# A fused decoder trunk on one core: VectorE's order in the differential heads, and what TensorE runs in the last two

## The chip, the cores and the metric

The kernel runs on one core of a Trainium2 chip. The metric is the device time of one execution in microseconds (us). Of the kernel before, three timed runs are shown: 712.58, 714.68 and 714.70, median 714.68 us.

## The reference

`x` is (1, 512, 1024) in float32, and the trunk has two layers.

```python
# layer 0: stick-breaking attention, 16 heads of 64
q, k, v, gate = split(rms_norm(x, g) @ w_in, 4)
x = x + (silu(gate) * stick_breaking_attention(q, k, v)) @ w_out
# shared keys and values of layer 1
k, v = split(rms_norm(x, kv_norm_g) @ w_kv, 2)       # 8 heads, keys 2 x 64, values 128
k = rope(rms_norm(k, k_norm_g))
# layer 1: differential attention
q, gate = split(rms_norm(x, g) @ w_in, 2)
q = rope(rms_norm(q, q_norm_g))
p = softmax(causal(q @ k.T / 8))                     # two maps (c = 0, 1) for each head
o = (p[0] - lam * p[1]) @ v
o = rms_norm(o, subln_g) * (1 - lam_init)
x = x + (silu(gate) * o) @ w_out
```

## The kernel before, in words

**Numbers.** Every matmul operand is kept as a rounded part (`_hi`) and the rest (`_lo`), and each product is three matmuls: hi x hi, hi x lo, lo x hi (`three`, L568 to L572). Weights come from HBM in slabs of 128x512. SyncE issues the loads (`slab`, L345), and each slab is split into hi and lo: GpSimd does both parts, or, for the slabs in `ACT_HI`, ScalarE the hi part (`slab_hi`, L935) and GpSimd the lo part (`split`, L464). In the differential stage the slabs stand in a ring of four slots (`RING_B`), so a slab can be split only when TensorE has used the slab four before it (semaphore `s_wu`), and loaded only when the slab four before it has been split (`s_w`).

**Stages.** First the stick-breaking layer, then the shared keys and values, then the differential stage (from L790 on TensorE), which is where the change lies. It has eight heads h = 0 to 7, each a pass over one 128-column block. Heads 0 and 1 stand apart, heads 2 to 5 are a loop (L896), heads 6 and 7 stand apart again (`late_head`, L879), and then comes the output projection (`project_out`, L730): 16 slabs `H_OUT` to `H_OUT + 15`, for each slab four tiles of 128 rows, eight output tiles in all.

**TensorE in head h of the loop** (`head`, L853): the scores of both maps into banks 0 to 5 (`scores_b`, L790); the q projection of head h + 2 into bank 6, and between its two slabs the spread of the output norms' roots of head h - 2 into bank 7 (`o_roots`, L812); the probabilities times values of head h - 1 into bank 7 (`attend_before`, L844, which waits for `s_og`, that is for VectorE's `o_scale(h - 2)`); the gate projection of head h into bank 6, and between its two slabs the sums of squares (`sums`, L756, which wait in `s_ot` for `o_times_gate(h - 1)`) and the transposes of the combined probabilities of head h (`turn_probs`, L820, which wait in `s_cm`). In heads 6 and 7 no q projection is left (`late_head`): scores, roots, attend, gate projection, sums, transposes.

**VectorE in head h** (`head`, L1544), in this order:

```python
for b in range(3): # maxima of a bank's scores from PSUM, then the bias of the exponentials (L1554, L1559)
q_add(h + 2)            # L1511, needs the swap of halves by four small DMAs (swap_halves, L400)
gate_log(h + KT)        # L1310
o_scale(h - 2)          # L1535, needs o_roots
combine((3, 2), 2, 4)   # L1572 to L1577: reciprocal, ratio, two strips of 512 and 384 columns
gate_silu(h + KT)       # L1316, then a wait for its own end (st.link)
q_low(h + 2)            # L1516
o_times_gate(h - 1)     # L1541, needs silu and ScalarE's output_square
combine((0, 1), 0, 8)   # strips of 128 and 256 columns, releases turn_probs
keep_hi(h - 2, ...); keep_lo(h - 2, ...)   # L1326, L1332: the gated output, split, for the projection
# mean squares, a root with ScalarE, Newton steps, then at_lo x3 (L1600), q_rotate(h + 3) (L1504, L1505)
```

`at_lo` of head h releases the scores of head h + 1 (`s_al`, L796).

**ScalarE in head h** (`head`, L1196): copy and absolute value of the gate from bank 6, exp and log of it (`gate_parts`, L1189, which waits for `s_ot`); the exponentials of bank 0; `q_square`; those of banks 2 and 3; `q_round`, which waits for `q_add`; `gate_exp`, which waits for `gate_log`; those of the last banks; `q_copy`; `output_square` (waits for attend, `s_pv`); the root; three copies of the transposed probabilities (L1223).

**GpSimd in head h**: the split of k for the next head (`key`, L521), two slab splits, the split of v (`value`, L526), two slab splits. A split is a cast (L479 or L493) and a subtraction (L481 or L495). At the end its order is H_OUT, H_OUT + 1, `value(7)`, H_OUT + 2 and the rest (L559 to L563).

Where the text gives a time as T6 + 5, T6 is the start of the scores of head 6. The functions that the diff touches, with the line numbers of the profile:

## Time and profile before

| | us |
|---|---|
| median of three runs | 714.68 |
| the profiled execution | 713.42 |
| its span in the trace | 712.0 |
| TensorE busy | 653.8 (92% of the span) |
| VectorE busy | 430.1 (60%) |
| ScalarE busy | 329.4 (46%) |
| GpSimd busy | 340.4 (48%) |
| mean granted clock of TensorE | 0.966 of full |
| chain that ended last: TensorE / VectorE / issue / ScalarE | 62% / 23% / 7% / 5% |

The span is what lies between the first and the last instruction; the execution's own time has 1.4 us more. A share of busy time is a mean over stages with different limits, so the argument goes stage by stage. A matmul's row shows its start and an overlapping duration; the distance from one start to the next is what it costs.

### The profile page before, as it was taken

What the parts mean: (1) busy time and instruction counts of PE and PEld (TensorE: products, weight loads), DVE (VectorE), ACT (ScalarE), POOL (GpSimd) and SP (SyncE); (2) the same over time, 40 slices, a digit from 0 to 9 for tenths busy, and PEclk for the clock granted to TensorE, in tenths of its full rate; (3) what the DMA queues carried; (4) which work ended last, traced back from release to release, by engine and by line L of the source; (5) the groups of instructions that cost most, each with busy time, mean ns of one, the idle gap of its engine ahead of it and who ended that gap; (6) DMA issues with size and microseconds to landing.
All of it is one profiled execution on the core that took longest, in us unless ns stands there. A gap on an engine that the chain in (4) does not pass through costs nothing.

```text
span 712.0 us, 10029 instructions
## 1 busy us (share of the span) xinstructions
PE 653.8 (92%) x3388; PEld 548.7 (77%) x3388; DVE 430.1 (60%) x683; ACT 329.4 (46%) x714; POOL 340.4 (48%) x325
## 2 busy tenths in 40 slices
PE   5999989999999999859798999998999889778898
PEld 4788778888888888758687888886877778667786
DVE  3400274775957758474937398237888998775421
ACT  4330555474754756632416544333654556443420
POOL 5554665544554442442551454558654574252241
PEclk9999999999999999989999999999999999876999
DMA  6222221212112110004121222233221111220241
GB/s 236 89 90 73 75 83 38 73 44 59 53 42 66 44 59 29 0 1 129 55 94 40 98 100 90 89 89 104 62 58 51 52 44 45 71 64 2 58 142 65
DMA packets 61773, 49.08 MB, mean 69 GB/s; under 512 B 7728, under 2 KB 48816, under 8 KB 61744
## 3 DMA queue, kind: packets, MB, share of 16 engines
q1 hardware_dynamic: 61744, 48.71, 22.5%
q8 instruction: 17, 0.28, 0.2%
q14 instruction: 12, 0.10, 0.0%
HBM read 44.50 MB, written 2.10 MB: 65 GB/s over the span
## 4 chain that ended last, share of the span: by engine, by line
PE 62%; DVE 23%; issue 7%; ACT 5%; DMA 2%; SPq 1%; DVEq 0%; ACTq 0%
PE bank L570 16%; PE bank L571 16%; PE bank L572 16%; PE bank L683 6%; DVE small L1554 3%; DVE hi L1354 3%; DVE lo L1359 2%; DVE sp L1348 2%; PE bank L668 2%; DVE ge L1310 1%; ACT ex L1027 1%; PE bank L807 1%; DVE ex L1435 1%; DMA xs<-in_x 1%; DVE v L1278 1%
## 5 line engine op out<-in xcount | busy, mean ns | idle before, releaser
L469 POOL TENSOR_TENSOR w_lo<-w_raw,w_hi 128x512 fp32r<-128x512 f32 x60 | 81.6, 1366 | 135.0 <-ACT w_hi L940 135.0
L481 POOL TENSOR_TENSOR w_lo<-w_raw,w_hi 128x512 fp32r<-128x512 f32 x100 | 139.0, 1390 | 8.0
L570 PE MATMUL bank<-w_hi,h_hi 128*128 128x512 f32 x320 | 128.6, 402 | 6.9 <-DVE xs L1416 4.1
L570 PE MATMUL bank<-h_hi,w_hi 128*128 128x512 f32 x320 | 131.4, 411 | 3.3 <-ACT q L1122 3.3
L479 POOL CAST w_hi<-w_raw 128x512 fp32r<-128x512 f32 x100 | 68.4, 684 | 131.9 <-PE bank L572 84.7
L571 PE MATMUL bank<-h_lo,w_hi 128*128 128x512 f32 x320 | 128.1, 400 | 0.0
L572 PE MATMUL bank<-h_hi,w_lo 128*128 128x512 f32 x320 | 127.7, 399 | 0.0
L572 PE MATMUL bank<-w_hi,h_lo 128*128 128x512 f32 x320 | 126.5, 395 | 0.0
L571 PE MATMUL bank<-w_lo,h_hi 128*128 128x512 f32 x320 | 126.1, 394 | 0.0
L940 ACT ACTIVATE w_hi<-w_raw 128x512 fp32r<-128x512 f32 x60 | 37.2, 627 | 90.0 <-PE bank L572 74.0
L570 PEld LDWEIGHTS bank<-w_hi,h_hi 128*128 128x128 f32 x320 | 61.1, 191 | 20.2 <-DVE xs L1416 4.5
L570 PEld LDWEIGHTS bank<-h_hi,w_hi 128*128 128x128 f32 x320 | 62.1, 194 | 16.9 <-ACT q L1122 3.9
L572 PEld LDWEIGHTS bank<-h_hi,w_lo 128*128 128x128 f32 x320 | 61.7, 193 | 14.0
L572 PEld LDWEIGHTS bank<-w_hi,h_lo 128*128 128x128 f32 x320 | 60.8, 190 | 13.4
L571 PEld LDWEIGHTS bank<-h_lo,w_hi 128*128 128x128 f32 x320 | 61.8, 193 | 11.9
L571 PEld LDWEIGHTS bank<-w_lo,h_hi 128*128 128x128 f32 x320 | 61.1, 191 | 12.4
L1348 DVE SCALAR_TENSOR_TENSOR sp<-bank,ex 128x512 f32<-128x512 f32 (+1 forms) x48 | 28.4, 591 | 47.5 <-ACT ex L1032 47.5
L1204 ACT ACTIVATE pr<-bank,small 128x512 f32<-128x512 f32 (+3 forms) x64 | 38.8, 614 | 11.8 <-DVE small L1559 11.8
L1365 DVE TENSOR_TENSOR lo<-ex,hi 128x512 fp32r<-128x512 f32 (+1 forms) x48 | 39.0, 866 | 7.4 <-ACT hi L1040 7.4
L683 PE MATMUL bank<-hi,neg_tri 128*128 128x512 f32 (+1 forms) x64 | 23.6, 380 | 14.5 <-DVE lo L1359 14.5
L1022 ACT ACTIVATE ex<-bank 128x512 f32<-128x512 f32 (+1 forms) x48 | 25.3, 528 | 23.3 <-PE bank L668 22.6
L1359 DVE TENSOR_TENSOR lo<-sp,hi 128x512 fp32r<-128x512 f32 (+1 forms) x48 | 35.4, 738 | 0.6
(175 smaller groups left out, 1220.7 us busy)
## 6 DMA issues: line engine op xcount, KB each, us to landing
w_raw<-in_a_w_in SPq DMA_DIRECT2D x64, 256.0 KB, 2.7
w_raw<-in_w_kv SPq DMA_DIRECT2D x32, 256.0 KB, 3.0
w_raw<-in_b_w_in SPq DMA_DIRECT2D x32, 256.0 KB, 2.8
w_raw<-in_a_w_out SPq DMA_DIRECT2D x16, 256.0 KB, 3.0
w_raw<-in_b_w_out SPq DMA_DIRECT2D x16, 256.0 KB, 2.9
xs<-in_x SPq DMA_DIRECT2D x4, 512.0 KB, 5.3
qrot<-qs SPq DMA_DIRECT2D x32, 64.0 KB, 2.0
out_x<-xs SPq DMA_DIRECT2D x8, 256.0 KB, 2.7
```

What stands on the lines that cost most here:

```text
L469: nc.gpsimd.tensor_tensor(w_lo[s][:, :], w_raw[s][:, :], w_hi[s][:, :].bitcast(F32), ALU.subtract).then_inc(s_w, 1)
L479: nc.gpsimd.tensor_copy(w_hi[s][:, :], w_raw[s][:, :]).then_inc(s_whi, 1)
L481: nc.gpsimd.tensor_tensor(w_lo[s][:, :], w_raw[s][:, :], w_hi[s][:, :].bitcast(F32), ALU.subtract).then_inc(s_w, 1)
L570: pe.matmul(o, ahi, bhi, start=start, stop=False, skip_group_check=True)
L571: pe.matmul(o, ahi, blo, start=False, stop=False, skip_group_check=True)
L572: return pe.matmul(o, alo, bhi, start=False, stop=stop, skip_group_check=True)
L683: mm = pe.matmul(bank[3 * h + b][:, cols(c, n)], (neg_tri if i == j else neg_one)[:, :], part[h][:, cols(STRIP[i][0], n)], start=False, st ...
L940: A(w_hi[s][:, :], w_raw[s][:, :], ACT.Copy).then_inc(s_whia, 1)
L1204: A(pr[c][:, cols(at, w)], bank[BANK_B[c, b]][:, cols(at - BANKS[b][0], w)], ACT.Exp, bias=tiny[:, 8 + 2 * i + c:9 + 2 * i + c], scale=mea ...
L1348: STT(out=sp[m // 3][:, seg], in0=bank[m][:, 0:BANKS[m % 3][1]], scalar=0.0, op0=ALU.max, in1=ex[m // 3][:, seg], op1=ALU.add).then_inc(s_ ...
L1359: TTN(lo[h][:, seg], sp[h][:, seg], hi[h][:, seg].bitcast(F32), ALU.subtract).then_inc(s_sl, 1)
L1365: TTN(lo[h][:, seg], ex[h][:, seg], hi[h][:, seg].bitcast(F32), ALU.subtract).then_inc(s_al, 1)
```

## The change

- VectorE's order in a head is now: maxima and biases, `o_scale`, `gate_log`, `combine((3, 2))`, `q_add`, `gate_silu`, `combine((0, 1))`, `o_times_gate`, `q_low`, `keep_hi`, `keep_lo`, and the rest as before. `gate_silu` no longer waits for its own end; it counts in a new semaphore `s_si`, for which `o_times_gate`, the stick-breaking layer's `gated_a` and ScalarE's `gate_parts` wait.
- ScalarE does `q_round` after the last exponentials and `q_copy`, and `gate_exp` earlier by that.
- In head 6 TensorE runs gate projection 6 before attend, and gate projection 7 behind the sums, with the transposes of head 6 between its slabs. In head 7 it runs no projection of a gate; in its place the first four slabs of the output projection are run tile by tile (`early_tile(0)` to `(3)`), each over k = 0 to 3, between the other steps. The output tiles have banks of their own (`OUT_BANK_B`), so no output tile waits for VectorE's addition.
- GpSimd splits the slabs H_OUT to H_OUT + 3 before `value(7)`.
- ScalarE and VectorE take their steps for gates 6 and 7 at the new places (`later`, `gate=False`). In head 6 ScalarE's `gate_parts(6)` stands ahead of `q_round` and `output_square`, and waits for `gate_silu(14)`.

The diff, cut to its core:

```diff
@@ -556,10 +560,10 @@
         value(KT - 2)
-        split(H_OUT)
-        split(H_OUT + 1)
+        for g in range(H_OUT, H_OUT + RING_B):
+            split(g)
         value(KT - 1)
-        for g in range(H_OUT + 2, N_ALL):
+        for g in range(H_OUT + RING_B, N_ALL):
             split(g)
@@ -587,15 +591,15 @@
-        def bulk_step(g, n0, k, src_hi, src_lo, freed, first):
+        def bulk_step(g, n0, k, src_hi, src_lo, freed=None, first=0, banks_of=range(8), tiles=range(TT)):
...
             whi, wlo = w_hi[slot_of(g)][:, :], w_lo[slot_of(g)][:, :]
-            for t in range(TT):
-                if k == 0 and n0 + t >= 6:
+            for t in tiles:
+                if freed and k == 0 and n0 + t >= 6:
                     pe.wait_ge(freed, first + n0 + t - 5)
-                mm = three(bank[(n0 + t) % 6][:, :], src_hi[:, k, cols(t * P, P)], src_lo[:, k, cols(t * P, P)],
+                mm = three(bank[(n0 + t) % 6 if freed else banks_of[n0 + t]][:, :], src_hi[:, k, cols(t * P, P)], src_lo[:, k, cols(t * P, P)],
                            whi, wlo, start=(k == 0), stop=(k == KT - 1))
...
@@ -876,17 +880,12 @@
-        def late_head(h, g, q=None):
-            scores_b(h, False)
-            o_roots(h - 2)
-            attend_before(h, 2)
-            pe.wait_ge(s_gc, h + KT)
-            pe.wait_ge(s_ga, h + KT)
-            project(g, h1_hi, h1_lo, bank[6][:, :])
-            sums(q, h - 1)
-            turn_probs(h)
+        def early_tile(t):
+            for k in range(RING_B):
+                pe.wait_ge(s_o, KT + k + 1)
+                bulk_step(H_OUT + k, 0, k, h2_hi, h2_lo, banks_of=OUT_BANK_B, tiles=(t,))
@@ -895,21 +894,45 @@
             head(i, 2)
-        late_head(KT - 2, H_GATES, KT - 1)
-        late_head(KT - 1, H_GATES + 2)
+        h = KT - 2
+        scores_b(h, False)
+        pe.wait_ge(s_gc, h + KT)
+        pe.wait_ge(s_ga, h + KT)
+        project(H_GATES, h1_hi, h1_lo, bank[6][:, :], between=lambda: o_roots(h - 2))
+        attend_before(h, 2)
+        sums(h + 1, h - 1)
+        pe.wait_ge(s_gc, h + KT + 1)
+        pe.wait_ge(s_ga, h + KT + 1)
+        project(H_GATES + 2, h1_hi, h1_lo, bank[6][:, :], between=lambda: turn_probs(h))
+        scores_b(KT - 1, False)
         pe.wait_ge(s_gc, 2 * KT)
         pe.wait_ge(s_ga, 2 * KT)
-        attend_b(KT - 1, 3 * KT, bank[6])
+        early_tile(0)
+        o_roots(KT - 3)
+        attend_before(KT - 1, 2)
+        pe.wait_ge(s_pe, 8 * KT - 6)
+        early_tile(1)
+        sums(o=KT - 2)
+        turn_probs(KT - 1)
+        early_tile(2)
+        attend_b(KT - 1, 3 * KT, bank[0])
         o_roots(KT - 2)
-        def last_sums():
-            pe.wait_ge(s_og, 2 * KT - 1)
-            sums(o=KT - 1)
-        def last_roots():
-            o_roots(KT - 1)
-        project_out(H_OUT, 2 * TT, {(0, 1): last_sums, (0, 3): last_roots})
+        early_tile(3)
+        bulk_step(H_OUT + 4, 0, 4, h2_hi, h2_lo, banks_of=OUT_BANK_B)
+        pe.wait_ge(s_og, 2 * KT - 1)
+        sums(o=KT - 1)
+        pe.wait_ge(s_o, 2 * KT - 2)
+        bulk_step(H_OUT + 5, 0, 5, h2_hi, h2_lo, banks_of=OUT_BANK_B)
+        o_roots(KT - 1)
+        for k in (KT - 2, KT - 1):
+            pe.wait_ge(s_o, KT + k + 1)
+            bulk_step(H_OUT + k, 0, k, h2_hi, h2_lo, banks_of=OUT_BANK_B)
+        for k in range(KT):
+            bulk_step(H_OUT + KT + k, TT, k, h2_hi, h2_lo, banks_of=OUT_BANK_B)
@@ -1188,14 +1211,16 @@
-            act.wait_ge(s_ot, h)
+            act.wait_ge(s_si, h + KT)
             gate_copy(used)
...
-        def head(h, first=False, gate=None, q_used=None, q_next=True):
-            if not first:
+        def head(h, first=False, gate=None, q_used=None, q_next=True, later=None):
+            if gate is not None:
                 gate_parts(h - 1, gate)
+            elif later is not None and h == KT - 1:
+                gate_parts(h, later)
             for b, strips in enumerate(((3,), (2, 0), (1,))):
@@ -1206,21 +1231,26 @@
                     q_square(h + 2)
-                if b == 1:
-                    if q_next:
-                        act.wait_ge(s_z, h * 6 + 54)
-                        q_round(h + 1)
-                    if not first:
-                        gate_exp(h + KT)
+                if b == 1 and gate is not None:
+                    gate_exp(h + KT)
             if q_used is not None:
                 q_copy(h + 3, q_used)
+            if later is not None and h == KT - 2:
+                gate_parts(h, later)
+            if q_next:
+                act.wait_ge(s_z, h * 6 + 54)
+                q_round(h + 1)
             if not first:
                 output_square(h - 1)
+            if later is not None and h == KT - 1:
+                gate_exp(h + KT + 1)
             c0, c1 = mean_cols(first, not q_next)
...
                 A(at_hi[:, cols(*BANKS[b])], bank[BANK_B[0, b]][:, 0:BANKS[b][1]], ACT.Copy).then_inc(s_ah, 1)
+            if later is not None and h == KT - 2:
+                gate_exp(h + KT + 1)
@@ -1231,11 +1261,9 @@
             head(i, gate=i * 4 + H_BODY, q_used=i * 4 + (H_BODY + 2))
-        head(KT - 2, gate=H_GATES)
-        head(KT - 1, gate=H_GATES + 2, q_next=False)
-        gate_parts(KT - 1, H_GATES + 4)
-        gate_exp(2 * KT)
-        output_square(KT - 1, bank[6])
+        head(KT - 2, gate=H_GATES, later=H_GATES + 2)
+        head(KT - 1, q_next=False, later=H_GATES + 4)
+        output_square(KT - 1, bank[0])
         slab_hi(H_OUT + 4)
@@ -1313,7 +1341,7 @@
             dve.wait_ge(s_gg, n)
-            st.link(TTN(silu[:, :], g32[:, :], ge[:, :], ALU.mult))
+            TTN(silu[:, :], g32[:, :], ge[:, :], ALU.mult).then_inc(s_si, 1)
...
@@ -1538,10 +1565,11 @@
             dve.wait_ge(s_oq, h + 1)
+            dve.wait_ge(s_si, h + (KT + 1))
             STT(out=ot[:, :], in0=o[:, :], scalar=gsub, op0=ALU.mult, in1=silu[:, :],
...
-        def head(h, n_before, q_next=True, q_after=True):
+        def head(h, n_before, q_next=True, q_after=True, gate=True):
             def biases(v, b):
@@ -1558,12 +1586,10 @@
                     in1=biases(means[:, 12:20], b), op1=ALU.mult).then_inc(s_nb, 1)
-            if q_next:
-                q_add(h + 2)
-            if n_before:
-                gate_log(h + KT)
             if n_before == 2:
                 o_scale(h - 2)
+            if gate:
+                gate_log(h + KT)
@@ -1579,16 +1605,21 @@
             combine((3, 2), 2, 4)
+            if q_next:
+                q_add(h + 2)
+            if gate:
+                gate_silu(h + KT)
+            combine((0, 1), 0, 8).then_inc(s_cm, 1)
             if n_before:
-                gate_silu(h + KT)
+                o_times_gate(h - 1)
             if q_next:
                 q_low(h + 2)
-            if n_before:
-                o_times_gate(h - 1)
-            combine((0, 1), 0, 8).then_inc(s_cm, 1)
             if n_before == 2:
...
                 keep_lo(h - 2, h + (KT - 1))
+            if not gate and n_before:
+                gate_log(2 * KT)
+                gate_silu(2 * KT)
             c0, c1 = mean_cols(not n_before, not q_next)
@@ -1609,26 +1640,27 @@
         q_rotate(2)
-        head(0, 0)
+        head(0, 0, gate=False)
         head(1, 1)
         with dve.Fori(2, KT - 2) as i:
-            st.enter(i, 2, 11)
+            st.enter(i, 2, 10)
             head(i, 2)
...
         head(KT - 2, 2, q_after=False)
-        head(KT - 1, 2, q_next=False, q_after=False)
+        gate_log(2 * KT - 1)
+        gate_silu(2 * KT - 1)
+        head(KT - 1, 2, q_next=False, q_after=False, gate=False)
         o_scale(KT - 2)
-        keep_output(KT - 2, 2 * KT - 1)
-        gate_log(2 * KT)
-        gate_silu(2 * KT)
-        o_times_gate(KT - 1, bank[6])
+        keep_hi(KT - 2, 2 * KT - 1)
+        o_times_gate(KT - 1, bank[0])
+        keep_lo(KT - 2, 2 * KT - 1)
         dve.wait_ge(s_sum, KT + 2)
...
         keep_output(KT - 1, 2 * KT)
-        add_residual(H_OUT, 8 * TT, 0)
-        add_residual(H_OUT, 8 * TT, 1)
+        add_residual(H_OUT, 8 * TT, 0, OUT_BANK_B)
+        add_residual(H_OUT, 8 * TT, 1, OUT_BANK_B)
 # ---- launch: one core; inputs and outputs as the reference has them
```

## Rows read from the trace of the kernel before

**Rows 1.** Busy time by head; columns: stretch, length, engines, PEclk, DMA share, GB/s
```profile
504.08:525.25 21.17, 19.25 (x117) 16.30 (x117) 19.02 (x33) 11.68 (x30) 12.73 (x12) 1.00 0.22 63
525.25:548.03 22.78, 21.35 (x122) 17.66 (x120) 20.04 (x35) 11.71 (x30) 12.42 (x12) 0.93 0.21 58
548.03:569.94 21.91, 19.89 (x121) 16.35 (x119) 18.82 (x33) 11.83 (x31) 12.04 (x12) 1.00 0.21 60
569.94:593.23 23.29, 21.44 (x121) 17.98 (x121) 21.53 (x36) 11.58 (x30) 12.73 (x12) 0.93 0.12 34
593.23:616.27 23.04, 21.21 (x122) 17.59 (x120) 19.11 (x34) 11.70 (x30) 10.19 (x10) 0.93 0.14 37
616.27:639.49 23.22, 15.93 (x98) 13.80 (x96) 18.65 (x32) 12.41 (x32) 12.78 (x12) 0.85 0.35 101
639.49:663.90 24.41, 20.74 (x104) 17.91 (x105) 13.05 (x29) 10.98 (x29) 5.87 (x6) 0.72 0.07 22
663.90:712.00 48.10, 45.22 (x207) 37.23 (x205) 12.99 (x21) 9.00 (x16) 15.50 (x12) 0.99 0.26 88
```

**Rows 2.** Timeline of PE, heads 3 and 4; columns: start us, us, engine, line
```profile
563.84 0.35 PE L765 MATMUL bank<-small,qsq 128*128 128x2 f32 x2 [1.18 <-DVE ot L1541]
...
575.75 0.60 PE L816 MATMUL bank<-ident,small 128*128 128x128 f32 x4
...
579.78 0.49 PE L570 MATMUL bank<-at_hi,vb_hi 128*128 128x512 f32 x1 [0.68 <-DVE og L1535]
...
585.86 0.35 PE L765 MATMUL bank<-small,qsq 128*128 128x2 f32 x2 [1.16 <-DVE ot L1541]
```

**Rows 3.** Timeline of DVE, heads 2, 4 and 7
```profile
540.36 2.12 DVE L1577 SCALAR_TENSOR_TENSOR pr<-pr,small 128x128 f32<-128x128 f32 x2
...
576.19 1.05 DVE L1511 TENSOR_TENSOR qc<-qc,qrot 128x512 f32<-128x512 f32 x1
577.16 1.78 DVE L1310 SCALAR_TENSOR_TENSOR ge<-g,ge 128x512 f32<-128x512 f32 x1
...
579.93 2.40 DVE L1577 SCALAR_TENSOR_TENSOR pr<-pr,small 128x512 f32<-128x512 f32 x2
...
584.98 0.73 DVE L1541 SCALAR_TENSOR_TENSOR ot<-bank,small,silu 128x512 f32<-128x512 f32 x1
...
585.82 1.06 DVE L1573 SCALAR_TENSOR_TENSOR small<-small 128x2 f32<-128x2 f32 x1
...
648.00 1.28 DVE L1577 SCALAR_TENSOR_TENSOR pr<-pr,small 128x512 f32<-128x512 f32 x2
```

**Rows 4.** Timeline of POOL, heads 4 and 6
```profile
576.78 1.61 POOL L481 TENSOR_TENSOR w_lo<-w_raw,w_hi 128x512 fp32r<-128x512 f32 x1
579.27 0.61 POOL L479 CAST w_hi<-w_raw 128x512 fp32r<-128x512 f32 x1 [0.88 <-PE bank L572]
...
583.00 1.51 POOL L495 TENSOR_TENSOR vb_lo<-v,vb_hi 128x512 fp32r<-128x512 f32 x1 [0.19 <-POOL vb_hi L493]
...
585.60 1.26 POOL L481 TENSOR_TENSOR w_lo<-w_raw,w_hi 128x512 fp32r<-128x512 f32 x1
...
620.69 0.63 POOL L479 CAST w_hi<-w_raw 128x512 fp32r<-128x512 f32 x1 [13.02 <-DMA w_raw<-in_b_w_in]
```

**Rows 5.** Waits of PE from 616.2 to 664 us: us in total, times, longest
```profile
PE bank L570 <- DVE og L1535: 7.0, 2, 5.2
PE bank L647 <- DVE at_lo L1600: 2.1, 1, 2.1
PE bank L570 <- ACT ge L1015: 1.8, 1, 1.8
```

**Rows 6.** Instructions by line from 450 us on, ScalarE's gate step
```profile
L1004 ACT ACTIVATE ge<-ge 128x512 f32<-128x512 f32 x8 | 5.1, 632 | 0.3
```

**Rows 7.** Timeline of PE, output projection: 38 tile steps from first to last
```profile
676.98 0.39 PE L570 MATMUL bank<-w_hi,h_hi 128*128 128x512 f32 x1
...
702.83 0.39 PE L570 MATMUL bank<-w_hi,h_hi 128*128 128x512 f32 x1
```

More of the change, by code:

```diff
@@ L99 @@
 R_HEAD = R_Q0 + 1
+OUT_BANK_B = [6, 1, 3, 5, 2, 4, 0, 7]
 def ring(g):
@@ L268, in build @@
     s_gg = sem("gate_sigmoid")
+    s_si = sem("gate_silu")
     s_o = sem("gated_output_split")
@@ L735, in project_out @@
                         pe.wait_ge(s_o, n0 + k + 1)
-                    bulk_step(g + half * KT + k, half * TT, k, h2_hi, h2_lo, s_x2, n0)
+                    bulk_step(g + half * KT + k, half * TT, k, h2_hi, h2_lo, s_x2 if n0 == 0 else None, n0, OUT_BANK_B)
                     if (half, k) in between:
@@ L1341, in gated_a @@
             dve.wait_ge(s_pv, p + 1)
+            dve.wait_ge(s_si, p + 1)
             TTN(og[:, :], bank[7][:, :], silu[:, :], ALU.mult).then_inc(s_og, 1)
@@ L1403, in _ @@
         with dve.Fori(1, KT - 1) as i:
-            st.enter(i, 1, 1)
             pair(i)
-            st.leave(KT - 2)
         pair(KT - 1, last=True)
@@ L1409, in _, with add_residual @@
         keep_output(KT - 1, KT)
-        def add_residual(g, m, half):
+        def add_residual(g, m, half, banks_of=range(8)):
             for n in range(half * TT, half * TT + TT):
@@ L1415, in add_residual @@
                 bulk_tile(dve, g + (n // TT + 1) * KT, m + n)
-                TTN(xs[:, t, seg], bank[n % 6][:, :], xs[:, t, seg], ALU.add).then_inc(s_x2, 1)
+                TTN(xs[:, t, seg], bank[banks_of[n]][:, :], xs[:, t, seg], ALU.add).then_inc(s_x2, 1)
         dve.wait_ge(s_par, 16 * 14)
@@ L1450, in _ @@
         st.link(last)
-        add_residual(G_OUT, 2 * TT, 0)
+        add_residual(G_OUT, 2 * TT, 0, [0, 1, 2, 3, 4, 5, 0, 1])
         dve.wait_ge(s_cs, 3)
@@ L1467, in _ @@
                     op1=ALU.subtract))
-        add_residual(G_OUT, 2 * TT, 1)
+        add_residual(G_OUT, 2 * TT, 1, [0, 1, 2, 3, 4, 5, 0, 1])
         norm_rows(1)
```

## The prediction, made before the change was run

> **What bounds the kernel now.** I read the page first: TensorE is busy for 92% of the span, and the chain that ended last is 62% TensorE and 23% VectorE. Then the busy times head by head [rows 1]: heads 2 to 5 take 21.91 to 23.29 us, and their granted clock is 1.00 or 0.93; head 6 falls to 0.85 and head 7 to 0.72, and only 15.93 of head 6's 23.22 us are busy. Then TensorE's timeline [rows 2]: in each loop head it waits some 0.7 us for `o_scale` before attend and 1.2 us for `o_times_gate` before the sums. At the end it waits 7.0 us for `o_scale`, 2.1 for `at_lo` and 1.8 for the gate's copy [rows 5]. So VectorE's chain sets the pace.
>
> VectorE is slow because it and GpSimd get in each other's way [rows 3, 4]. The two long strips of `combine` cost 1.28 us in head 7, where GpSimd is idle (648.00), and 2.40 in head 4 (579.93). `gate_log` (577.16, 1.78 us) ends 0.55 us after GpSimd's subtraction from 576.78 ends at 578.39; the tiny ratio at 585.82 takes 1.06 us, to within 0.02 us of the end of the subtraction from 585.60. The reverse holds too: the subtraction from 576.78 takes 1.61 us behind `q_add` (576.19, 1.05), against 1.26 at 585.60. Where both are ready they take turns: 540.36 shows two short strips at 2.12 us. Steps with an operand in PSUM stay short, such as `o_times_gate` (584.98, 0.73). The Trainium skill, SBUF — State Buffer, section "SBUF: two separate sides", has this as a lock held for a whole instruction. By that rule, which the rows above bear out, a new order doesn't remove the blocking; it only deals it out anew.
>
> **Part 1, VectorE's order in heads 1 to 5.** I walk head 4 through the new order with a lock passed by turns. Unblocked steps of 512 columns cost 0.55 us here and 0.68 in full, GpSimd's cast 0.5 to 0.6, its subtraction 1.15 to 1.3. The roots are spread by 576.35 [rows 2]; `o_scale` runs to 577.1, so TensorE's 0.7 us wait for it is gone. `gate_log` waits for GpSimd's subtraction (now to 578.07) and ends at 578.6; the ratio ends at 579.0; the first long strip ends at 579.65, ahead of the cast of 579.27 [rows 4], which ends at 580.15; the second strip 580.55; subtraction 581.7; `q_add` 582.25; cast of v 582.75; `gate_silu` 583.3; subtraction of v 584.45; the second ratio 584.5; cast 585.05; strip of 128 at 585.2; subtraction 586.35; strip of 256 at 586.65; `o_times_gate` 587.3. Before it ended at 585.71 [rows 3]. So what TensorE's sums wait for comes 1.6 us later: ahead of it now stands `combine((0, 1))`, two locked strips and a ratio, in place of `q_low`, one locked step; and `combine((0, 1))`, which before ran beside the sums, was hidden there. `q_low` is hidden in its new place behind the sums (1.9 us). TensorE, which gets to that wait 0.8 us earlier, idles 3.5 us instead of 1.2. ScalarE's later `q_round` ends by 583, long before `q_low`; its `output_square` by 583.6, before `o_times_gate`. Both cost nothing while VectorE is that late; without this cover 0.6 us each. The link dropped from `gate_silu` is worth under 0.1 us, and in the stick-breaking layer nothing, since VectorE waits there for ScalarE anyway.
>
> Per head 1.5 us. Then the clock. A mean of 0.93 over 23 us is 3.3 us at the half rate, and with TensorE busy 1.6 us lost at most; from the sums to the next head takes 7.37 us in head 4 and 6.10 in head 3 [rows 1, 2], so 1.3 is what it costs. Heads 2, 4 and 5 pay it already. With 3.5 us of idle ahead of the sums I take it that heads 1 and 3 (1.00 now) pay it too. Heads 1 to 5: 5 x 1.5 + 2 x 1.3 = **+10.1**. Bounds: if `o_times_gate` comes as early relative to its head as some turn-taking allows (the short strips run without the lock going over between them, 0.9 us less) and the clock falls as often as now, 5 x 0.6 = +3; with no lock at all the waits vanish, -2 us a head, **-10**; if the half rate lasts through the next scores (about 6 us of work at half rate, 3 lost, against 1.3), +19. I take the middle, nearest to the rows of head 4. The Trainium skill, TensorE: Matmul & The Clock Gate, section "HAM oscillation — how this bites in real kernels", says that a loop whose waits let the clock fall pays the fall in every round. Head 3 of the trace does not bear that out at 1.2 us of idle; by the rule all rounds pay, by the rows alone as few as three of five, and the sum would be 2.6 us lower.
>
> **Part 2, head 6.** TensorE's work at full clock from T6 to the end is 76.9 us: a slab's tile step is 25.85 / 38 = 0.68 us [rows 7], so 64 of them 43.5, two projections 11.1, scores 5.8, three attends 6.1 (an estimate from their columns), sums, transposes and roots 7.3, and 3.1 behind the last matmul. It takes 95.7 us now [rows 1], so 18.8 are lost. The change fills the 5.2 us wait with gate projection 6, and opens another: after attend, at T6 + 11.1, the sums need `o_times_gate(5)`. GpSimd is held up by a load until T6 + 4.4 (620.69) [rows 4], so its splits, `key(7)`, `value(6)` and now four output slabs in a row all fall on VectorE's chain: `gate_log` T6 + 8.9, long strips 11.6, `q_add` 12.2, silu 13.2, the second ratio 14.4, its strips 16.6. On ScalarE, `gate_parts(6)` waits for that silu, and behind it stand `q_round` and `output_square(5)`: six steps of some 0.6 us [rows 6] from T6 + 13.2, to 16.9. So `o_times_gate(5)` ends at T6 + 17.6 and TensorE has idled 6.6 us, with some 2 more lost to the clock. Head 7 then starts at T6 + 28.2, with both gate projections done.
>
> **Part 3, head 7 and the output.** Early tiles of 2.7 us each stand where TensorE waited. Tile 0 needs slab H_OUT + 3, whose slot is free when head 7 starts: split by + 2.4, needed at + 5: hidden. The wait for `o_scale(5)` goes; `at_lo` of head 7 is ready about 0.9 us after tile 2: left. `s_wu` of a slab now comes with tile 3 only, so slab H_OUT + 4 is split at the last moment: + 0.2. Lost in heads 6 and 7: 6.6 + 2 + 0.9 + 0.2, and 0.6 for small gaps, makes 10.3 against 18.8: **-8.5** (bounds: 4.5 if head 6 idles 10 us, 11 if its collisions are few). Moving the banks costs and gains nothing: VectorE's additions (four in 2.7 us) were hidden. No load is added or moved; H_OUT + 2 and + 3 are split earlier.
>
> **Sum**: the profiled execution's 713.42 (span 712.0 and 1.4 around it) + 10.1 - 8.5 = 715.0. The median of the runs is 1.3 above that execution; half of that gives **715.5 us**. About 0.3% (2.1 us) is what a measurement of this kernel can tell from no change.
>
> **Rivals.** A, the forecast: the heads give back what the end gains, 712.5 to 717: 0.36. B, faster: the new order deals the collisions out well, `o_times_gate` moves by 0.6 or less, and the loop costs 0 to 3: 713.4 - 8.5 + 0 to 3 = 705 to 708, or 710 to 712 with 6: 0.32. For it: head 2 reached `o_times_gate` over 1 us sooner than head 4 by such a turn. Against: the new order puts more locked work ahead of it. Should the lock not bind in these places, 695. C, slower: TensorE's clock. If 3.5 us of idle and the sums keep the rate at half through the next projection and scores, each head loses up to 1.8 more, 713.4 + 10.1 + 5 x 0.9 - 8.5 = 719.5, up to 724; it decides from 0.5 us more per head: 0.28. D, the change doesn't do what it says: GpSimd, with four splits ahead of `value(7)` and VectorE in its way, brings the slabs late and TensorE waits for early tiles as long as before: -2 instead of -8.5, 721.5: 0.04.
>
> **Chances and range.** Faster 0.32, same 0.36, slower 0.32. The range of 8 in 10 is 706 to 722; forecast A alone has 712.5 to 717.
>
> **What would show it.** Right: no wait of L570 on `o_scale` in the loop, a wait of L765 on L1541 of 3 us or more in heads 2 to 5, a granted clock at or below 0.93 in each of them, heads of 24 to 25 us; a wait of 6 to 7 us before the sums of head 6, and from the scores of head 7 to the end 59 us instead of 72.5. Wrong: loop heads under 23 us (B), a clock of 0.87 or less in them (C), waits of `bulk_step` on GpSimd's L481 in head 7 (D).

## The result, and the profile after

The median is 729.72 us (727.3 to 730.65, 4 runs) against 714.69 of the kernel before (4 runs): ratio 1.0207, 95% interval 1.0169 to 1.0244. The change makes the kernel 15.0 us **slower**. I had forecast 715.5 us and a range of 706 to 722: wrong. The profiled execution has a span of 725.9 us instead of 712.0, and a mean granted clock of 0.955 instead of 0.966.

The page of the kernel after, TensorE's rows of the slices and the chain that ended last:

```profile
PE   5999899999999999689889999997898889859998
PEclk9999999999999999989999999998898998887999
PE 65%; DVE 22%; ACT 5%; issue 5%; DMA 2%; SPq 1%; POOL 0%; DVEq 0%; ACTq 0%
```

TensorE is still busy for 91% of the span, and these rows alone would not say what went wrong. What it waits for in the differential stage does (the kernel after, waits of PE from 480 to 726 us; total, times, longest):

```profile
PE bank L769 <- DVE ot L1569: 24.1, 6, 8.1
PE bank L574 <- ACT q L1145: 2.1, 1, 2.1
PE bank L831 <- DVE pr L1603: 2.0, 1, 2.0
PE bank L574 <- DVE h_lo L1360: 1.0, 1, 1.0
PE bank L574 <- DVE og L1562: 0.8, 1, 0.8
```

The first row is the sums' wait for `o_times_gate` (now L1569). The waits for `o_scale` in the loop are gone, as the change meant; this one has taken their place and more. By head (the kernel after, busy time by stretch, columns as in [rows 1]; first head 0, last head 7 with all behind it):

```profile
482.40:505.60 23.20, 19.11 (x98) 15.88 (x96) 18.29 (x29) 9.03 (x25) 14.01 (x13) 0.85 0.31 85
505.60:531.12 25.52, 21.93 (x117) 19.10 (x116) 18.94 (x31) 11.90 (x30) 12.88 (x12) 0.87 0.17 47
531.12:557.45 26.33, 22.84 (x121) 19.52 (x120) 20.33 (x34) 11.93 (x30) 12.46 (x12) 0.87 0.20 54
557.45:582.13 24.68, 21.20 (x121) 18.13 (x120) 20.33 (x34) 11.93 (x30) 12.46 (x12) 0.93 0.18 50
582.13:608.44 26.31, 22.86 (x121) 19.47 (x120) 20.33 (x34) 11.93 (x30) 12.46 (x12) 0.87 0.13 35
608.44:633.29 24.85, 22.77 (x122) 19.70 (x120) 18.85 (x34) 11.91 (x30) 10.64 (x10) 0.86 0.10 27
633.29:665.29 32.00, 23.86 (x122) 20.45 (x120) 21.18 (x33) 13.79 (x34) 14.82 (x14) 0.79 0.26 82
665.29:725.90 60.61, 55.79 (x285) 45.83 (x283) 27.12 (x49) 18.67 (x43) 20.15 (x16) 1.00 0.23 74
```

Against [rows 1]: up to head 1's start +1.5 us; heads 1 to 5 127.7 instead of 112.2, **+15.5**; head 6 32.00 instead of 23.22, **+8.8**; head 7 to the end 60.6 instead of 72.5, **-11.9**. Together +13.9, the difference of the spans. TensorE's busy time in heads 1 to 5, the first number behind each length, grows from 103.1 to 111.6 us for the same work, its idle time from 9.1 to 16.1. The granted clock, 1.00 in two of the heads 1 to 5 before, is now 0.86 or 0.87 in four of them and 0.93 in the fifth.

**Where o_times_gate went.** The timeline of DVE, kernel after, heads 4 and 6:

```profile
588.48 0.69 DVE L1562 TENSOR_TENSOR og<-ot,bank 128x512 f32<-128x512 f32 x1 [0.22 <-PE bank L820]
589.08 1.62 DVE L1338 SCALAR_TENSOR_TENSOR ge<-g,ge 128x512 f32<-128x512 f32 x1
...
591.08 1.63 DVE L1603 SCALAR_TENSOR_TENSOR pr<-pr,small 128x512 f32<-128x512 f32 x2
592.64 1.76 DVE L1538 TENSOR_TENSOR qc<-qc,qrot 128x512 f32<-128x512 f32 x1
594.33 1.09 DVE L1344 TENSOR_TENSOR silu<-g,ge 128x512 f32<-128x512 f32 x1
...
596.62 2.12 DVE L1603 SCALAR_TENSOR_TENSOR pr<-pr,small 128x128 f32<-128x128 f32 x2
598.66 0.74 DVE L1569 SCALAR_TENSOR_TENSOR ot<-bank,small,silu 128x512 f32<-128x512 f32 x1
...
645.16 1.75 DVE L1538 TENSOR_TENSOR qc<-qc,qrot 128x512 f32<-128x512 f32 x1
...
649.10 2.13 DVE L1603 SCALAR_TENSOR_TENSOR pr<-pr,small 128x128 f32<-128x128 f32 x2
651.45 0.75 DVE L1569 SCALAR_TENSOR_TENSOR ot<-bank,small,silu 128x512 f32<-128x512 f32 x1 [0.23 <-issue]
```

In head 4 every step stands within 0.2 us of where the prediction's walk put it (its times plus the 12.19 us by which this head starts later): `gate_log` ends at 590.70 (walk 590.79), `q_add` at 594.40 (594.44), the short strips at 598.74 (598.84), `o_times_gate` at 599.40 (599.49). `o_times_gate` ends 17.27 us behind the head's start, and a strip pair of 128 and 256 columns, 0.75 us when nothing is in its way (e7 below), takes 2.12.

**What the wait does to the clock.** The timeline of PE, kernel after, end of head 4:

```profile
599.55 0.35 PE L769 MATMUL bank<-small,qsq 128*128 128x2 f32 x2 [3.42 <-DVE ot L1569]
...
600.43 0.56 PE L769 MATMUL bank<-small,qsq 128*128 128x2 f32 x2
...
605.59 0.63 PE L574 MATMUL bank<-h_hi,w_hi 128*128 128x512 f32 x1
...
607.29 0.40 PE L575 MATMUL bank<-h_lo,w_hi 128*128 128x512 f32 x1
...
608.44 0.33 PE L651 MATMUL bank<-mask_b,ident_r 128*128 128x128 f32 x2
```

0.9 us after the wait the pairs of the sums go from 0.35 to 0.56 us, and the projection's matmuls take 0.63 us instead of 0.40 until 607. The busy times by stretch show the granted clock at 1.00 up to 600, 0.61 from 600 to 602, 0.50 from 602 to 606: TensorE is at the lower of its two levels (1.2 instead of 2.4 GHz) for some 6.8 us. From the sums to the next head it needs 8.89 us here; in head 4 of before it was 7.37, and 6.10 in head 3.

### The profile page after: what moved, and what is told of

It is laid out like the page before. It is cut to its first block, busy times and chain, and to the rows that moved or that the text cites. A ratio compares the mean times of both kernels' runs of the same rounds, so it can differ in the third digit from the quotient of the medians.

```text
span 725.9 us, 10034 instructions
## 1 busy us (share of the span) xinstructions
PE 661.3 (91%) x3388; PEld 557.3 (77%) x3388; DVE 435.5 (60%) x683; ACT 330.7 (46%) x714; POOL 341.2 (47%) x325
## 4 chain that ended last, share of the span: by engine, by line
PE 65%; DVE 22%; ACT 5%; issue 5%; DMA 2%; SPq 1%; POOL 0%; DVEq 0%; ACTq 0%
PE bank L574 16%; PE bank L575 15%; PE bank L576 15%; PE bank L687 6%; DVE hi L1383 3%; PE bank L831 2%; DVE pr L1603 2%; DVE sp L1377 2%; PE bank L672 2%; DVE lo L1388 2%; PE bank L811 2%; DVE qc L1538 2%; PE bank L772 1%; PE bank L769 1%; ACT ex L1050 1%
## 5 line engine op out<-in xcount | busy, mean ns | idle before, releaser
L575 PEld LDWEIGHTS bank<-h_lo,w_hi 128*128 128x128 f32 x320 | 62.4, 195 | 11.9
L575 PEld LDWEIGHTS bank<-w_lo,h_hi 128*128 128x128 f32 x320 | 61.1, 191 | 12.3
L769 PE MATMUL bank<-small,qsq 128*128 128x2 f32 x64 | 13.8, 298 | 24.1 <-DVE ot L1569 24.1
```

What stands on the lines that cost most here:

```text
L575: pe.matmul(o, ahi, blo, start=False, stop=False, skip_group_check=True)
```

## The experiments

The kernels of a pair are compared through the kernel before on the same chip: the ratios are to it. Lengths of heads, clocks and waits are read from each kernel's windows and TensorE timeline as above, that is from one execution: the fastest of ten in e1 (706.05 us), the slowest of ten in e4 (718.84), the slowest but one of ten in e10 (715.34). The ratios rest on all runs.

### e1: the new end, with VectorE's old order in heads 0 to 5

```diff
@@ DVE head(h, ...)
+            old = q_after
+            if old and q_next:
+                q_add(h + 2)
+            if old and gate:
+                gate_log(h + KT)
...
+            if old:
+                if q_next:
+                    q_low(h + 2)
+                if n_before:
+                    o_times_gate(h - 1)
             combine((0, 1), 0, 8).then_inc(s_cm, 1)
...
```

`q_after` is true in heads 0 to 5 only. The same steps at their new places are switched off there, and ScalarE's `q_round` goes back to its old place too.

> Heads 0 to 5 go back to VectorE's and ScalarE's order of before; heads 6, 7 and the output projection stay as changed. Theory 1 (the order costs some 17 us in heads 0 to 5, the new end gives 3): heads 1 to 5 back to 21 to 23.5 us each, head 6 near 31 instead of 23.2, from the scores of head 7 to the end near 60 instead of 72.5; 711 to 713 us. Theory 2 (the new end is what makes the kernel slower, through GpSimd's four splits): 722 us or more.

Measured: 710.87 us (10 runs), ratio 0.9955 [0.994, 0.997]; clock 1.00 in three of the heads 1 to 5. Head 6 takes 30.49 us with a wait of 8.05, head 7 to the end 60.50. Against the 95.7 us of heads 6 and 7 before, the end is worth -4.7 in the profile, where I had said -8.5; by the ratio of all runs the kernel gains 0.45%, 3.2 us.

### e2: VectorE's and ScalarE's new order, with the old end

```diff
@@ DVE head(h, ...)
-            if q_next:
-                q_add(h + 2)
...
             combine((3, 2), 2, 4)
+            if q_next:
+                q_add(h + 2)
             if n_before:
                 gate_silu(h + KT)
-            if q_next:
-                q_low(h + 2)
+            combine((0, 1), 0, 8).then_inc(s_cm, 1)
             if n_before:
                 o_times_gate(h - 1)
-            combine((0, 1), 0, 8).then_inc(s_cm, 1)
+            if q_next:
+                q_low(h + 2)
```

The first `...` leaves out that `o_scale` goes ahead of `gate_log`; ScalarE's later `q_round` isn't shown.

> The kernel before with VectorE's new order (and ScalarE's later q_round) in all heads, and TensorE's end as before. Theory 1: heads 1 to 5 at 24.7 to 26.3 us as in the changed kernel, 730 to 734 us. Theory 2: 714 to 717 us.

Measured: 731.9 us (4 runs, 724.45 to 735.71), ratio 1.0256 [1.022, 1.0293]; waits for `o_times_gate` of 3.60, 3.43, 3.42, 3.43 and 2.09 us in heads 1 to 5. The two halves add up within their intervals: +2.6% of the order and -0.45% of the end are the +2.1% of the whole. The loss lies in the order.

### e3: o_times_gate ahead of combine((0, 1)) again

```diff
+            if n_before:
+                o_times_gate(h - 1)
             combine((0, 1), 0, 8).then_inc(s_cm, 1)
-            if n_before:
-                o_times_gate(h - 1)
```

> The changed kernel with o_times_gate ahead of combine((0, 1)) again, the rest of the new order kept. Theory 1: the step that TensorE's sums wait for ends 2 us or more sooner in each head, their wait falls from 3.4 us to 1.2 or less, the clock falls less often, heads 1 to 5 at 22 to 23.5 us; 713 to 718 us. A rival (the loss comes from the place of q_add and o_scale, not of combine((0, 1))): the wait stays over 2.5 us and the time over 725.

Measured: 709.6 us (4 runs), ratio 0.9936 [0.9913, 0.9959]. The sums wait some 0.5 us (0.67 in head 1) instead of 3.4, the transposes 0.5; heads 1 to 5 take 20.26 to 22.54 us, at 1.00 in three of them and 0.92 in two. The place of this one step is the whole loss. Against e1, which has the old order throughout and the same end (0.9955), the rest of the new order may be a small gain, but the intervals overlap.

### e4: the waits filled, with the order left as it is

```diff
@@ PE head(h, n_before), ahead of the sums
+                if n_before:
+                    pe.wait_ge(s_pe, h * 8 + 8)
+                    for _ in range(14):
+                        pe.matmul(bank[1][:, :], ident_r[:, :], h1_hi[:, 0, :], start=True, stop=True,
+                                  skip_group_check=True)
```

> The changed kernel with 14 matmuls of 512 columns into bank 1 (free there, and their result is never read) ahead of the wait of the sums, heads 1 to 5. If what I mis-sized is TensorE's clock (2.8 us a head instead of 1.3): granted clock 0.97 or more in heads 1 to 5, from the start of the sums to the next scores 6 us instead of 7.3 to 8.9, the heads 1.3 to 2.8 us shorter, 717 to 722 us. If the clock isn't it, the heads stay at 24.7 to 26.3 us and the time at 730.

Measured: 716.16 us (10 runs), ratio 1.0002 [0.9984, 1.0021]. Fourteen matmuls that nobody reads occupy TensorE through the wait in heads 1 to 5; `o_times_gate` comes no earlier, and the kernel is 13.6 us faster than after. Heads 1 to 5 take 117.8 us instead of 127.7, at 1.00 in three of them and 0.93 in heads 2 and 4. So most of the loss is not the wait but the clock after it. What is left over before's 112.2 us is the length of the wait, less what the clock gives back beyond before (two heads pay here, three there). The 0.97 that I had asked for in every head did not come: in head 2 TensorE stands still for 0.33 us ahead of the sums, and its clock is at 0.50 from 551 to 553 all the same.

### e5: GpSimd out of the way

```diff
@@ split(g)
+            nw = 16 if H_BODY <= g < H_OUT else 512
-            nc.gpsimd.tensor_copy(w_hi[s][:, :], w_raw[s][:, :]).then_inc(s_whi, 1)
+            nc.gpsimd.tensor_copy(w_hi[s][:, 0:nw], w_raw[s][:, 0:nw]).then_inc(s_whi, 1)
```

The subtraction is cut in the same way. Left out is the split of 496 of the 512 columns of the slabs that the differential heads use.

> The changed kernel, but GpSimd splits only 16 of the 512 columns of the weight slabs of the differential heads (the rest of those slabs keeps older contents, so q and gates are computed from wrong weights); its splits of k and v stay whole. Theory 1 (VectorE's steps are long because GpSimd holds what both need): the long strips of combine back to 1.3 to 1.9 us, o_times_gate at about T + 14 instead of T + 17.3, the wait of the sums under 1 us, heads 1 to 5 at 19.5 to 21.5 us with the new order unchanged, under 712 us. Rival (the order is slow in itself, whatever GpSimd does): the wait stays above 2.5 us and the heads at 24 us or more.

Measured: 688.74 us, one execution. The timeline of DVE, head 4:

```profile
566.99 0.68 DVE L1339 SCALAR_TENSOR_TENSOR ge<-g,ge 128x512 f32<-128x512 f32 x1
...
569.25 0.69 DVE L1539 TENSOR_TENSOR qc<-qc,qrot 128x512 f32<-128x512 f32 x1
569.85 0.69 DVE L1345 TENSOR_TENSOR silu<-g,ge 128x512 f32<-128x512 f32 x1
...
571.69 0.75 DVE L1570 SCALAR_TENSOR_TENSOR ot<-bank,small,silu 128x512 f32<-128x512 f32 x1
572.36 1.79 DVE L1544 TENSOR_TENSOR q_lo<-qc,q_hi 128x512 fp32r<-128x512 f32 x1
```

and the busy times of that head:

```profile
560.05:579.17 19.12, 19.12 (x121) 16.61 (x120) 16.43 (x36) 11.83 (x30) 6.97 (x12) 1.00 0.15 41
```

The same instructions of VectorE, in the same order and with the same tiles, take 0.68 or 0.69 us instead of 1.62 (`gate_log`), 1.76 (`q_add`) and 1.09 (`gate_silu`), `o_times_gate` ends 12.39 us behind the head's start instead of 17.27, none of the heads 1 to 5 waits for it, and every head of the loop takes 19.12 us. `q_low`, which here meets the split of v that was left whole, still takes 1.79. This confirms the prediction's reading of [rows 3, 4]: VectorE's long steps are the time of GpSimd's splits beside them. By the Trainium skill, SBUF — State Buffer, section "SBUF: two separate sides", the two engines share one lock. The traces agree, and the price of it in the heads 2 to 5 is 5.6 to 7.2 us each (24.68 to 26.33 against 19.12), the clock that it brings down included. The new order is not slow by itself: with nothing in its way it would be hidden.

### e6: ScalarE takes q_round and output_square(5) ahead of gate_parts(6)

```diff
@@ ACT head(h, ...)
-            if later is not None and h == KT - 2:
-                gate_parts(h, later)
             if q_next:
                 act.wait_ge(s_z, h * 6 + 54)
                 q_round(h + 1)
             if not first:
                 output_square(h - 1)
+            if later is not None and h == KT - 2:
+                gate_parts(h, later)
```

> The changed kernel, but in head 6 ScalarE does q_round and output_square(5) ahead of gate_parts(6). If that order is what holds back o_times_gate(5): it starts right behind the short strips; but these end only 0.23 us before it in the changed kernel, so the wait of 8.1 us before the sums of head 6 falls by 0.2 to 0.5 us only, and GpSimd's splits are the cause. If ScalarE's order is the cause: 2 us or more less.

### e7: GpSimd splits H_OUT and the rest only when the sums of head 6 have run

```diff
@@ POOL, ahead of the splits of H_OUT to H_OUT + 3
+        pool.wait_ge(s_sum, KT)
```

> The changed kernel, but GpSimd waits for the sums of head 6 before it splits the first output slabs. If the early splits cost VectorE its time in head 6: the second ratio and the short strips lose the 2 to 3 us that they are blocked now, and, ScalarE's order left as it is, o_times_gate(5) comes when output_square(5) ends, some 0.3 us sooner; together with the order of e6 it would be 2 to 3 us. Head 6 31.5 us instead of 32.0; head 7 unchanged (early tile 0 still finds its slabs). If the splits come too late for early tile 0, a new wait of TensorE on GpSimd in head 7.

Measured: 730.65 us for e6 and 728.27 for e7, one execution each, read by head 6 alone. Its wait is 6.85 us in e6 and 7.78 in e7, against 8.14 after. Why each helps so little shows in head 6 of the kernel after. The timeline of ACT there:

```profile
647.95 0.60 ACT L1022 ACTIVATE g<-bank 128x512 f32<-128x512 f32 x1 [4.23 <-DVE silu L1344]
...
650.27 0.61 ACT L1156 ACTIVATE q_hi<-qc 128x512 fp32r<-128x512 f32 x1
650.79 0.57 ACT L1258 ACTIVATE osq<-bank 128x512 f32<-128x512 f32 x1
```

and of POOL:

```profile
639.43 0.61 POOL L483 CAST w_hi<-w_raw 128x512 fp32r<-128x512 f32 x1 [16.58 <-DMA w_raw<-in_b_w_in]
...
645.00 1.35 POOL L499 TENSOR_TENSOR k_lo<-k,k_hi 128x512 fp32r<-128x512 f32 x1 [0.18 <-POOL k_hi L497]
...
648.99 0.60 POOL L483 CAST w_hi<-w_raw 128x512 fp32r<-128x512 f32 x1
649.67 1.27 POOL L485 TENSOR_TENSOR w_lo<-w_raw,w_hi 128x512 fp32r<-128x512 f32 x1
650.89 0.80 POOL L483 CAST w_hi<-w_raw 128x512 fp32r<-128x512 f32 x1
```

`o_times_gate(5)` (651.45) needs two things: `combine((0, 1))`, which the splits of the output slabs hold up to 651.2, and `output_square(5)`, which the gate's four steps on ScalarE hold up to 651.36. Each edit removes one and leaves the other. The timeline of DVE in e7:

```profile
650.72 0.75 DVE L1604 SCALAR_TENSOR_TENSOR pr<-pr,small 128x128 f32<-128x128 f32 x2
653.88 0.75 DVE L1570 SCALAR_TENSOR_TENSOR ot<-bank,small,silu 128x512 f32<-128x512 f32 x1 [2.42 <-issue]
```

The strips are back at 0.75 us, and `o_times_gate` stands for 2.42 us more ("issue" here: ScalarE's square, which nothing in the row names). Of the little that each gives, most is not its own doing. In e6 and e7 GpSimd's first split of the head, which waits for a load (639.43 above), starts 4.2 and 4.3 us behind the head's start instead of 6.1. The turns fall differently, and `q_add` ends at 12.6 instead of 13.6 us, ahead of everything that the two edits touch. In e6 the short strips end 1.0 us earlier with it, which leaves 0.3 of its 1.3 us, the size that I had expected; in e7 `gate_silu` ends 0.4 us earlier, which is all that e7 gives.

From head 7 to the end e7 takes 60.59 us as after does, so splitting the output slabs that early buys nothing.

### e8: the repairs together

e3, e6 and e7, and in head 0 `q_add` behind `combine((0, 1))`:

```diff
@@ DVE head(h, ...)
-            if q_next:
+            if q_next and n_before:
                 q_add(h + 2)
...
             combine((0, 1), 0, 8).then_inc(s_cm, 1)
+            if q_next and not n_before:
+                q_add(h + 2)
```

> The changed kernel with o_times_gate ahead of combine((0, 1)) (as e3), q_add of head 0 behind combine((0, 1)), ScalarE's order of e6 and the splits of e7. Theory: heads 1 to 5 as in e3 (20 to 22.6 us), head 0 1.5 us shorter, head 6 at 26 to 28 us instead of 30.5, head 7 as before: 704 to 708 us, faster than both kernels. If head 6's wait has another cause, 708 to 710.

Measured: 706.15 us (4 runs), ratio 0.9882 [0.9855, 0.991]: faster than both kernels. Head 6 takes 26.65 us with a wait of 4.25, head 0 19.98. Heads 1 to 5 take 110.28 us, a little more than in e3 (108.17). The sixth head's wait is 3.9 us shorter than in after (0.4 of it because `gate_silu` ends that much sooner behind the head's start), where e3's order alone gave 0.5 (its wait is 7.64), e6's edit 1.3 and e7's 0.4. `o_times_gate(5)` now starts at 630.03, right behind `gate_silu` (629.90): e3's order takes the short strips out of its way and e6's takes the square out. With the strips behind it, e7's edit can no longer help it by way of the strips, and no run leaves that edit out; what it is worth in e8 is open.

### e9: e8, with the rest of the waits filled

Three matmuls as in e4 ahead of the sums of heads 1 to 5, eighteen ahead of those of head 6.

> This is e8_together (706.15 us, span 703.8) with small matmuls that nothing reads put ahead of the sums: three in the heads 1 to 5, eighteen in the sixth. Theory (what is left of the waits costs its own length and also the clock after it): granted clock 0.97 or more in the heads 1 to 6, those heads at 20 to 21.5 us instead of 20.4 to 23.6, the sixth at 25 to 26 instead of 26.65, the whole at 697 to 703 us. Rival (waits as short as those left in e8_together do not lower the clock; something else does): 706 us, and the dummies may cost 0.3 us a head, so up to 708.

Measured: 702.81 us (4 runs), ratio 0.982 [0.9777, 0.9864], the fastest of the kernels that leave nothing out, though its interval just overlaps e8's. Heads 1 to 5 together take 108.75 us instead of e8's 110.28, but two of them stay at 0.92. The theory asked for 0.97 or more, so it holds in part. In head 6 the edit pays nothing (its windows, head 6 and from head 7 to the end):

```profile
613.63:639.22 25.59, 23.56 (x139) 19.86 (x139) 22.65 (x35) 13.39 (x33) 17.31 (x16) 1.00 0.34 102
639.22:702.20 62.98, 57.50 (x284) 47.24 (x284) 26.92 (x50) 18.92 (x43) 17.96 (x15) 0.97 0.21 72
```

At full clock the head is 1.06 us shorter, and head 7 begins with a new wait of 2.03 us for `at_lo`: the two together take 88.6 us against 88.1 in e8. There VectorE's chain is the bound, not the clock.

### e10: the kernel before, with five such matmuls ahead of the sums

> The kernel before, with five small matmuls that nothing reads ahead of the sums of the heads 1 to 5. Theory (the 1.2 us that TensorE waits there is what lowers the clock to 0.93 in the heads 2, 4 and 5): these heads at 1.00 and shorter by 1.3 us each, the whole at 710 to 711 us. Rival (the drops come from elsewhere in the head, such as the waits in the head before): 714 to 716 us and the same three heads at 0.93.

Measured: 712.55 us (10 runs), ratio 0.9938 [0.9908, 0.9969], between the theory (710 to 711) and its rival (714 to 716). The waits for `o_times_gate` are gone from heads 1 to 5, but three of them (1, 3 and 4 now) are still at 0.93. So in these the wait of 1.2 us is not what lowers the clock, as the rival had it, though not in the three heads that it named. The 3 us by which the median is below before's suggest that the filling helps in some executions. In head 3 of this kernel (timeline of PE):

```profile
566.04 1.29 PE L868 MATMUL bank<-h_hi,ident_r 128*128 128x512 f32 x5
567.38 0.35 PE L765 MATMUL bank<-small,qsq 128*128 128x2 f32 x2
...
569.24 2.18 PE L827 MATMUL bank<-ident,pr 128*128 128x128 f32 x10
571.08 0.78 PE L570 MATMUL bank<-h_hi,w_hi 128*128 128x512 f32 x1
```

and its granted clock around them:

```profile
567.00:569.00 2.00, 1.96 (x17) 1.66 (x15) 1.93 (x5) 0.00 (x0) 1.31 (x2) 1.00 0.00 0
569.00:571.00 2.00, 2.00 (x12) 1.97 (x12) 1.36 (x5) 0.45 (x3) 0.00 (x0) 0.63 0.00 0
```

TensorE stands still for nothing here; the clock falls behind the sums, 16 matmuls of one or two columns in 1.8 us. That the sums cause it isn't shown: head 2, at 1.00, has the same ones. Why in this head and not in that one is left open.

### e11: e1 with the edits of e6 and e7

> The end alone (e1_tail_alone, 710.87 us), with ScalarE's order of e6_square_first and the later splits of e7_splits_later. Theory (the sixth head's wait has two causes, both named by those runs): the sixth head at 27 to 29 us instead of 30.5, the whole at 707.5 to 710. If it comes to 706 or less, VectorE's order by the chain is worth nothing in e8_together; if it stays at 710 or above, the order is worth 4 us or more there. Rival (e8_together's short sixth head comes from VectorE's order): the sixth head stays at 30 us and the whole at 710 to 711.

Measured: 708.93 us (7 runs), ratio 0.9911 [0.9882, 0.9941]; head 6 at 29.26 us with a wait of 5.70, a little above what the theory gave it. Head 6 has the new order here as in e1, whose wait is 8.05, so the edits of e6 and e7 together take 2.35 us off it; 0.9 of this is that `gate_silu` happens to end that much sooner. The old order with the repaired end against e8: head 6 is 2.6 us longer (e8 has `o_times_gate` ahead of the strips there), but the intervals of the ratios overlap. The best estimate of what VectorE's new order is worth in e8's form is 0.3%; that it is worth anything isn't shown.

## Why the prediction was wrong

**What bounds the kernel.** Right, and now shown: VectorE's chain, made slow by GpSimd's splits (e5).

**Part 1, the walk.** Right. I said that `o_times_gate` ends 17.36 us behind head 4's start and that TensorE idles 3.5 us; it was 17.27 and 3.42. I said that the wait for `o_scale` goes and that `q_low` is hidden; both hold. e3 shows that `combine((0, 1))` ahead of `o_times_gate` is the whole cause, as the walk had it.

**Part 1, the clock: the step that failed.** "1.3 is what it costs", once a head, added in the two heads that did not pay yet: 2.6 us. I had carried over the price of the fall in the kernel before [rows 1, 2] to waits of 3.5 us. The busy time of heads 1 to 5 says what the clock cost: 8.5 us in place of my 2.6. The idle time grows by 7.0, where I had 7.5. In four of the five heads the low level now lasts some 6.8 us, twice what it was in heads 2, 4 and 5 before, and the sums, taken as unaffected, slow down with it. So the stretch from the sums to the next head takes 8.7 to 8.9 us in heads 1, 2, 4 and 5 and 7.28 in head 3, against 6.10 at full clock in head 3 of before: 2.6 to 2.8 us lost in four heads, not 1.3. e4 measures it by itself: 9.9 us in the same heads, of which about 1.3 is that there one head fewer pays than before. Rival C named this mechanism, with a chance of 0.28, and its sign, a clock of 0.87 or less, came in four of the five heads, but it was priced at 0.9 us a head more (it was 1.2), and my bound for the low level lasting into the scores (+19) was never carried into the range.

**What sets the size of that price is open.** The prediction's "in each loop head" a wait of 1.2 us for `o_times_gate` was misread. The trace of before has it in heads 1, 3, 4 and 5, and only 4 and 5 pay. Head 2 pays without it; it has 0.66 us ahead of the transposes. Rows of before (PE), of e2's head 5, whose wait is 2.09 us, and of e8's head 3, whose wait is 0.51 us (windows):

```profile
542.54 1.31 PE L827 MATMUL bank<-ident,pr 128*128 128x128 f32 x10 [0.66 <-DVE pr L1577]
...
607.27:628.95 21.68, 19.58 (x121) 16.61 (x120) 17.95 (x34) 11.69 (x30) 10.63 (x10) 1.00 0.12 32
...
549.46:573.09 23.63, 22.70 (x121) 19.16 (x120) 19.94 (x35) 11.69 (x30) 12.47 (x12) 0.86 0.20 57
```

In the kernel after, head 5 pays in full (0.86) with a wait of 2.06 us, and head 3 pays half (0.93) with 3.45. So the length of the wait is not all that decides. In the Trainium skill, TensorE: Matmul & The Clock Gate, section "HAM oscillation — how this bites in real kernels", the rule is that a loop whose waits let the clock fall pays in every round. My sum followed it, with all five heads paying; it was the price of a round that was too low. The traces of the kernel after agree: all five heads pay, at waits of 2.06 to 3.60 us. At 1.2 us they don't: heads 1 and 3 of before are at 1.00.

**Head 0 was not costed.** `q_add` stands ahead of its `combine((0, 1))` too, and its transposes wait 2.03 us for the strips (L831 in the waits above). Head 0 takes 23.20 us instead of 20.31, but starts 1.4 us earlier (482.40 instead of 483.77), so up to head 1's start it is +1.5 us. e8, with that step moved back, has head 0 at 19.98 us; part of the difference is the clock's, since e6 and e7, with after's head 0, have 21.63 and 22.11.

**Part 2, head 6.** I said an idle of 6.6 us and a length of 28.2; it was 8.14 and 32.00. `o_times_gate(5)` ends 18.9 us behind the head's start (652.20) where I had 17.6. The step that slipped is `q_add`: I had it end at T6 + 12.2, 0.6 us behind the long strips, and it ends at 13.6 (646.91), 1.75 us long beside GpSimd's subtraction of k (645.00, above). The silu, ScalarE's six steps and the short strips then follow at the distances I gave. That is 1.3 us. A part of it is the load that holds up GpSimd: I had its end at T6 + 4.4, it came at T6 + 6.1 (639.43, above), and e6 and e7, where it came at 4.2 and 4.3, have `q_add` end at 12.6. The other 2.5 are the clock: the busy times by stretch show it at 0.50 to 0.56 from 648 to 662, and the 9.6 us of these in which TensorE works lose some 4.7, where I gave 2.

**Part 3, head 7 and the output.** Said 59 us, measured 60.61, at a clock of 1.00: the fill works. -11.9 us in place of -13.5; the slabs came in time (rival D falls), the two waits left are 0.78 and 1.04 us.

**The sum.** Of the 12.3 us by which the profiled execution (713.42 + 13.9 = 727.3) is above the 715.0 of the prediction's sum, heads 1 to 5 make 5.4, head 6 3.8, head 0 1.5 and the end 1.6. The other 1.9 us are that the median lies 2.4 us above the profiled execution, not 0.5. The range was too narrow at the top because all four errors have one sign: an idle TensorE costs its length and then the clock.

## What to carry to other kernels

When a change makes TensorE wait longer ahead of small matmuls, price the wait and the clock behind it apart, and let the range hold a slow stretch twice as long as the one measured; here waits of 2.1 to 3.6 us came with slow stretches of some 6.8 us in four heads of five, against 3.4 us in three of five before. Before moving a step ahead of another on a shared chain, ask which of the two releases the engine that sets the pace: the place of one step made 20 us here (729.72 against 709.6). If two causes hold up one step, test them together, since each edit alone gave 1.3 us or less here and together 3.9. And before an edit is given the credit, see whether the steps ahead of it ran as before.

## What the runs showed of the hardware that was not expected

- Filling a wait with matmuls that nobody reads gave 13.6 us back without bringing anything forward (e4).
- TensorE's clock falls behind 16 matmuls of one and two columns in 1.8 us, with the engine never idle ahead of them (e10, head 3; in head 2 it doesn't fall), and such matmuls slow down with it, from 0.35 to 0.56 us a pair, though they have hardly a column to stream.
- The clock differs between profiles of the same loop: with waits of 3.45 us in each head, heads 2 to 4 are at 0.87, 0.93 and 0.87 in the kernel after and at 0.81 three times in e6, which changes only ScalarE's order in head 6: 82.0 us against 77.3. A few us between two profiles can be this alone.
- GpSimd's splits cost VectorE's chain 4.9 us from a head's start to the end of `o_times_gate` (17.27 against 12.39, e5), though GpSimd is busy for only half of a head (12.46 of 26.31 us).
